# Eight differential attention heads: the gates of a head are computed one head later, the filler is spread 32 or 40 pieces to a head, and tanh, low halves and weight splits change places

## What is computed

```python
h = rms_norm_2(x, norm_g)
(c_glu, c_gate, d_q, d_k, d_v, d_gate, x_q, x_gate, merge) = split(h @ w_in)
u = a * sigmoid(b)              # a, b = split(c_glu): the GLU, then a convolution of 31 taps
u = conv(u, dw) + dw_b
q, k = rms_norm_2(d_q), rms_norm_2(d_k)          # per head: two halves m of 64
s = q @ k.T * scale - slope * dist               # causal
a = softmax(s[0]) - lam * softmax(s[1])
o = rms_norm_2(a @ v, subln_g) * (1 - lambda_init) * silu(d_gate)
```

## Time and profile before

| what | us |
|---|---|
| three runs: median (lowest to highest) | 1282.93 (1280.54 to 1284.0) |
| the profiled execution, its own time | 1289.19 |
| its span from first to last instruction | 1287.4 |
| TensorE busy in the span | 1215.9 (94%) |
| VectorE busy | 867.2 (67%) |
| ScalarE busy | 604.0 (47%) |
| mean granted TensorE clock | 0.973 |

### The profile page before, as it was taken

How to read it: one execution, slowest core, us unless ns; L and a number is a source line. 1 busy time by engine, 2 the same in 40 slices (tenths; PEclk the granted TensorE clock), 3 DMA queues, 4 the chain that set the end, 5 groups by cost and what they waited for, 6 DMA issues and landing times. The chain is left out here.

```text
span 1287.4 us, 17196 instructions
## 1 busy us (share of the span) xinstructions
PE 1215.9 (94%) x6530; PEld 1027.2 (80%) x6530; DVE 867.2 (67%) x1433; ACT 604.0 (47%) x1085; POOL 63.9 (5%) x62
## 2 busy tenths in 40 slices
PE   5999999998889999999999989999999899999998
PEld 5998888886689997777777766788887688788888
DVE  5887666757747246777977796588777668763341
ACT  6644364544546455664666455332564321752230
POOL 2039000000000000000000000000000000000001
PEclk9989999999989999999999999999999899999999
DMA  9965222110055322122112213223321422332211
GB/s 356 357 226 169 73 66 66 53 47 17 23 218 202 99 83 73 42 66 82 66 33 66 82 49 131 78 87 103 94 66 50 146 67 99 98 99 98 99 66 50
DMA packets 34290, 130.24 MB, mean 101 GB/s; under 512 B 4000, under 2 KB 4256, under 8 KB 33696
## 3 DMA queue, kind: packets, MB, share of 16 engines
q1 hardware_dynamic: 30672, 111.69, 26.2%
q0 software_dynamic: 3248, 17.14, 3.6%
q10 hardware_dynamic: 288, 0.31, 0.1%
HBM read 122.83 MB, written 6.29 MB: 100 GB/s over the span
## 5 line engine op out<-in xcount | busy, mean ns | idle before, releaser
L433 PE MATMUL bank<-hl,wh 128*128 128x512 f32 x880 | 365.7, 416 | 8.0 <-ACT th L1062 5.3
L434 PE MATMUL bank<-hh,wl 128*128 128x512 f32 x880 | 348.6, 396 | 0.0
L435 PE MATMUL bank<-hh,wh 128*128 128x512 f32 x880 | 348.6, 396 | 0.0
L1015 ACT ACTIVATE wh<-raw 128x1024 fp32r<-128x1024 f32 x187 | 192.1, 1054 | 205.3 <-PE bank L435 193.1
L1647 DVE TENSOR_TENSOR wl<-raw,wh 128x1024 fp32r<-128x1024 f32 x187 | 227.0, 1239 | 85.4 <-ACT wh L1015 84.6
L433 PEld LDWEIGHTS bank<-hl,wh 128*128 128x128 f32 x880 | 168.9, 192 | 46.9 <-issue 13.2
L435 PEld LDWEIGHTS bank<-hh,wh 128*128 128x128 f32 x880 | 168.6, 192 | 37.4
L434 PEld LDWEIGHTS bank<-hh,wl 128*128 128x128 f32 x880 | 169.0, 192 | 35.2 <-issue 4.4
L2078 DVE SCALAR_TENSOR_TENSOR ca<-u,vt,ca 128x512 f32<-128x512 f32 x232 | 157.9, 745 | 0.0
L433 PE MATMUL bank<-wl,hh 128*128 128x256 f32 (+1 forms) x352 | 101.8, 289 | 3.1 <-DVE hl L2333 2.4
L434 PE MATMUL bank<-wh,hl 128*128 128x256 f32 (+1 forms) x352 | 100.0, 284 | 0.0
(11 more groups left out here) (315 smaller groups left out, 1971.7 us busy)
## 6 DMA issues: line engine op xcount, KB each, us to landing
raw<-in_chunks SPq DMA_DIRECT2D x195, 512.0 KB, 3.7
ada_a<-in_chunks SPq DMA_DIRECT2D x8, 512.0 KB, 12.8
ada_b<-in_chunks SPq DMA_DIRECT2D x8, 512.0 KB, 12.8
x<-in_x POOLq DMA_DIRECT2D x4, 512.0 KB, 10.7
mem_scratch<-kvm POOLq DMA_DIRECT2D x1, 2048.0 KB, 8.2
x<-in_x POOLq DMA_DIRECT2D x1, 2048.0 KB, 9.5
x_scratch<-x POOLq DMA_DIRECT2D x1, 2048.0 KB, 6.6
kvm<-mem_scratch POOLq DMA_DIRECT2D x1, 2048.0 KB, 8.7
```

Of the source, the lines that this page charges most:

```text
L433: pe.matmul(o, a[0], b[1], start=start, stop=False, **kw)
L434: pe.matmul(o, a[1], b[0], start=False, stop=False, **kw)
L435: return pe.matmul(o, a[0], b[0], start=False, stop=stop, **kw)
L1015: act.activation(wh[:, SLOT[nxt]], raw[:, RAW_SLOT[nxt]], ACT.Copy).then_inc(s.w_hi, 1)
```

## The change

Seven edits, all in the stage of the eight heads:

1. The gate `dg` of head j becomes filler of head j + 1, ahead of that head's `gb` and `ga`; `dg` of head 7 stays in head 7, last.
2. Head 0 has 32 pieces instead of 40 and head 7 has 32 instead of 24; both give 8 to each tile.
3. At tt = 0 the turn of the previous head's last unit is two pieces later on TensorE.
4. ScalarE does its tanh ahead of the exponentials: of `dg(j - 1)` at tt = 2, of `gb(j)` at tt = 3 (before: behind them, `gb` at tt = 2, `dg` at tt = 3). In head 7 these are at tt = 1 and 2.
5. The high and low of the transposed probabilities come directly behind the exponentials and behind `prob`, ahead of weight splits, readouts and roots.
6. On VectorE the GLU of head j moves from tt = 3 to tt = 0 of head j + 1, the gate from tt = 3 to tt = 2, the mix from ahead of `prob` to behind it, and the output's low from tt = 3 to tt = 0 of the next head. In head 7 the mix and both output halves stay at tt = 3, behind `prob`.
7. Four taps move from tt = 2 to tt = 1; head 1 has four taps fewer, and the later stage runs 10 instead of 9 behind each projection chunk.

```diff
-    CHUNKS += [("gb", _j), ("ga", _j), ("dg", _j)]
+    CHUNKS += ([("dg", _j - 1)] if _j else []) + [("gb", _j), ("ga", _j)] + ([("dg", 7)] if _j == 7 else [])
...
-                    at, half = (10 * tt, 5) if j < 7 else ((0, 8, 12, 16)[tt], (4, 2, 2, 4)[tt])
+                    at, half = (10 * tt, 5) if 0 < j < 7 else (8 * tt, 4)
...
-                    if tt < 3 and 4 * j + tt > 0:
+                    if tt in (1, 2):
                         diff_turn(4 * j + tt - 1)
                     pieces(fill, at + half, 2)
-                    if tt == 3:
+                    if tt in (0, 3) and 4 * j + tt > 0:
                         diff_turn(4 * j + tt - 1)
...
+                    if j and tt == (2 if j < 7 else 1):
+                        tanh_of(("dg", j - 1)).then_inc(s.tanhed, 1)
+                        th_free[0] = ("dg", j - 1)
                     if tt == 3:
                         if j < 7:
                             act.wait_ge(s.qn_done, 2 * j + 4)
                             split_head(j + 1, ("D", u_, 1))
+                    if tt == (3 if j < 7 else 2):
+                        banks.empty(tanh_of(("gb", j)), ("gb", j))
+                        th_free[0] = ("ga", j)
...
+                    if u_ > 0:
+                        diff_pt_hi(u_ - 1)
...
+            ahead(("ga", 7))
             gate_of(("dg", 7))
             diff_pt_hi(31)
...
+                    if tt == 0 and j > 0:
+                        glu(j - 1)
+                    if (j, tt) == (7, 3):
+                        glu(7)
...
-                    if tt == 3 and j > 0:
-                        diff_mix(j - 1)
+                    if tt == 0 and j > 1:
+                        dve.wait_ge(s.mixed, j - 1)
+                        split_o(j - 2, 7 + j)
                     if tt < 3:
-                        conv(4, j)
+                        conv(4, j if tt else j - 1)
...
+                    if u_ > 0:
+                        diff_pt_lo(u_ - 1)
...
-            branch("d", diff_tail, lambda: conv(9, 8))
+            branch("d", diff_tail, lambda: conv(10, 8))
```

More of the change, by code:

```diff
@@ L771, in _ @@
             for j in range(8):
-                fill = ([("dq", j + 1), ("dk", j + 1)] if j < 7 else []) + [("gb", j), ("ga", j), ("dg", j)]
+                fill = [("dq", j + 1), ("dk", j + 1)] if j < 7 else []
+                fill += ([("dg", j - 1)] if j else []) + [("gb", j), ("ga", j)] + ([("dg", 7)] if j == 7 else [])
                 for tt in range(4):
-                    at, half = (10 * tt, 5) if j < 7 else ((0, 8, 12, 16)[tt], (4, 2, 2, 4)[tt])
+                    at, half = (10 * tt, 5) if 0 < j < 7 else (8 * tt, 4)
                     pieces(fill, at, half)
@@ L1448, in _ @@
                     if tt == 0 and j > 0:
-                        ahead(("dg", j - 1))
+                        ahead(("ga", j - 1))
                     if tt < 2 and j < 7:
@@ L1454, in _ @@
                         square_q(tt)
[L1455 to L1461, removed]
+                    if tt == 2 and j < 7:
+                        roots_together(([("sub", j - 1)] if j else []) + [("dns", 2 * j + 2 + i) for i in range(2)],
+                                       norms[:, 0:3 if j else 2, :])
                     if tt == 2:
                         split_v(dv[:, :, j * P:j * P + P], ("DO", j - 1) if j else ("PO", 15))
-                        ahead(("gb", j))
[L1465 to L1470, removed]
+                    if tt == 2 and j == 7:
+                        roots_together([("sub", 6)], norms[:, 2:3, :])
+                    if j and tt == (2 if j < 7 else 1):
+                        ahead(("dg", j - 1))
+                    if tt == (3 if j < 7 else 2):
+                        ahead(("gb", j))
+                    if tt == 3 and j > 0:
+                        split_o(j - 1, last=("wp", 3, 1), mixed=j)
+            ahead(("ga", 7))
             gate_of(("dg", 7))
@@ L2085, in conv, with glu @@
                         dve.tensor_tensor(u[:, j, PAD:], ca[:, 0, :], ca[:, 1, :], ALU.add).then_inc(s.conv_done, 1)
+            def glu(j):
+                key = ("ga", j)
+                banks.wait_empty(dve, ("gb", j))
+                banks.wait_full(dve, key)
+                banks.empty(dve.scalar_tensor_tensor(u[:, j, PAD:], th[:], 1.0, bank(key)[:], ALU.add, ALU.mult), key)
             def diff_pt_lo(u_):
@@ L2114, in _ @@
                            .then_inc(s.negmax, 1)
+                    if j and tt == (2 if j < 7 else 1):
+                        if j > 1:
+                            dve.wait_ge(s.mixed, j - 1)
+                        gate_to(("dg", j - 1), gj[:], False)
                     if tt == 3 and j < 7:
@@ L2132, in _ @@
                        .then_inc(s.prob_ready, 1)
+                    if u_ > 0:
+                        diff_pt_lo(u_ - 1)
                     if tt == 0 and j > 0:
-                        banks.wait_full(dve, ("dg", j - 1))
-                        ahead(("dg", j - 1))
+                        banks.wait_full(dve, ("ga", j - 1))
+                        ahead(("gb", j - 1))
+                        ahead(("ga", j - 1))
                     if tt < 2 and j < 7:
@@ L2139, in _ @@
                         ahead(key)
[L2140 to L2145, removed]
                     if tt == 2:
                         split_v(6 + j, dv[:, :, j * P:j * P + P])
[L2148 to L2157, removed]
+                        if j < 7:
+                            norm_q(0, v("dqn"), ("dns", 2 * j + 2))
+                            norm_q(1, v("dkn"), ("dns", 2 * j + 3))
+                    if tt == 1:
+                        conv(4, j)
+                    if j and tt == (2 if j < 7 else 1):
+                        ahead(("dg", j - 1))
+                    if tt == 3 and j > 0:
+                        diff_mix(j - 1)
+                    if (j, tt) == (7, 3):
+                        dve.wait_ge(s.mixed, 7)
+                        split_o(6, 15)
+                    if (j, tt) == (7, 2):
+                        banks.wait_full(dve, ("gb", 7))
+                        ahead(("gb", 7))
+            ahead(("ga", 7))
             gate_to(("dg", 7), gj[:])
```

## The result

The changed kernel takes 1265.89 us in the median of four runs (1264.09 to 1269.03), the kernel before 1283.47 in the same job; the ratio is 0.9854 with an interval of 0.983 to 0.9878. In a later job it took 1267.49 against 1283.3 (0.9861, 0.9832 to 0.989). Forecast were 1263 and 20 less; it is 16 to 18 less. The profiled execution took 1266.38 (span 1264.6).

What follows compares the result with a forecast made beforehand. TensorE, busy 94% of the span, waited mostly for VectorE's low at the turns. Gains of 15.6 + 7 + 0.95 less 0.8, 1.2 and 1.5 gave 20.0, from 1282.93 to 1262.9, said as 1263; range 1256 to 1272.

Steps and rivals of the forecast that it cites:

- The chain at the boundary: From tile 2 to the next head's turn: VectorE's low ends at 17.2 instead of 20.35, the turn comes at 19.4.
- The boundaries: Seven turns between heads no longer wait for VectorE's low: 15.6 us gained.
- Head 0: At head 1's start, behind a head 0 with fewer pieces, a new wait for the tanh: 0.8 us lost once.
- Inside head 7: Eight more pieces partly cover head 7's two waits: 1.15 left against 2.1, 0.95 us gained.
- The end: Behind head 7, in front of diff_values(7): a wait of 3.6 against 2.4 before, 1.2 us lost.
- Waits in sum: TensorE's waits over the stage of the heads: 20.1 to 5.6, 14.6 us less.
- The clock: Lower-clock stretches behind the stalls go, 7 us back; one returns behind the last wait, 1.5 us lost.
- The rival in which the stalls go and the clock doesn't come back: Boundary stalls vanish but the lower-clock stretches stay in the runs: gain 14.5, 1268.4 us, chance 25%.
- the forecast's own range: Whole kernel: the forecast itself holds from 1259.5 to 1267 us, chance 52%.
- The difference between 1289.19 and the median: Kernel before: runs without a profile 6.3 us faster than the profiled execution, about the 7 the clock costs in it.

Runs made afterwards that it cites:

- The tanh experiment: Changed kernel with the tanh of gb at tile 3 put back behind the exponentials in heads 0 to 6: 1275.1 us, ratio 0.9915 to before.
- the links: Changed kernel with three or eight extra multiplications of prob by 1.0 on VectorE, ahead of the low at tile 3 of heads 0 to 6: 1270.2 and 1289.1 us.
- the two single edits of the kernel before: Kernel before with prob and low ahead of mix and gate at tile 3: 1283.9 us; or with tile 0's turn two pieces later: 1275.6 us.
- the kernel with all three order edits: Kernel before with low first at tile 3, turn two pieces later, and every high and low ahead of splits and readouts: 1273.6 us.
- The first experiment: Changed kernel with the high and low of unit 31 ahead of weight splits and gate behind head 7: 1260.5 us; again 1260.7.
- The low-first run: Kernel before with prob and the low made ahead of the mix and gate on VectorE at tile 3: 1283.9 us, ratio 0.9999.
- the kernel with the turn later: Kernel before with the turn at tile 0 two pieces later on TensorE: 1275.6 us, ratio 0.9941.
- three links: Changed kernel with three extra multiplications of prob by 1.0 on VectorE ahead of the low at tile 3, heads 0 to 6: 1270.2 us.
- eight links: Changed kernel with eight extra multiplications of prob by 1.0 on VectorE ahead of the low at tile 3, heads 0 to 6: 1289.1 us.

## Why the prediction was right, and where it was off

**The chain at the boundary: shown.** Counted from VectorE's first maximum of head 4's tile 2 (633.71 here), the timeline of the changed kernel, VectorE:

```profile
642.63 0.69 DVE L1793 TENSOR_TENSOR vv<-dv,vv 128x512 fp32r<-128x512 f32 x1 [2.94 <-ACT vv L1237]
...
645.70 1.28 DVE L2126 TENSOR_REDUCE stat<-bank 128x1 f32<-128x512 f32 x2
...
648.93 0.17 DVE L2145 RECIPROCAL stat<-stat 128x2 f32<-128x2 f32 x1
...
650.51 0.55 DVE L1843 TENSOR_TENSOR ptl<-bank,pth 128x384 fp32r<-128x384 f32 x1
...
652.36 0.68 DVE L2099 SCALAR_TENSOR_TENSOR u<-th,bank 128x512 f32<-128x512 f32 x1
```

ScalarE and TensorE:

```profile
635.70 0.69 ACT L1035 ACTIVATE norms<-bank,sc 128x512 f32<-128x512 f32 x1
636.49 1.28 ACT L1042 ACT_TABLE_LOAD   x1
637.78 1.49 ACT L1042 ACTIVATE norms<-norms 128x1536 f32<-128x1536 f32 x1
...
646.51 0.60 ACT L1063 ACTIVATE th<-bank 128x512 f32<-128x512 f32 x1
```

```profile
647.32 0.41 PE L433 MATMUL bank<-hl,wh 128*128 128x512 f32 x1
...
653.08 0.60 PE L628 MATMUL bank<-cst,prob 128*128 128x128 f32 x4
```

`vv` is at 8.9 (forecast 8.75), the maxima at 12.0 (11.8), the reciprocal at 15.2 (15.05), the low ends at 17.35 (17.2), the GLU begins at 18.65 (18.5), the turn at 19.4 (19.4). All of VectorE is 0.15 later than forecast, because the first table load stands 0.79 behind the mean's start and not 0.62. So the spares are 2.0 at the turn, 1.3 at the GLU, and 0.2 at the tanh, which ends at 13.4 for a piece at 13.6. The tanh experiment and the links put a price on the last two. The load is 1.29 before its activation here too, and no drain shows; by the Trainium skill ("ScalarE: Activation LUTs", What ACT_TABLE_LOAD costs) there would be 1.38 more to each, and the trace disagrees.

**The boundaries: 15.6 forecast, 15.6 measured** (all seven waits are gone). What the prediction didn't see is how the edits hang together. It credited the gain to mix, gate and GLU leaving the chain; the two single edits of the kernel before show that each alone passes a part of the wait, or most of it, to the next turn. The timeline of the first shows the three splits in front of the late low there, and the kernel with all three order edits has no such wait. So the low ahead of the splits, to which the prediction gave no value, was most likely needed as well; the first two edits together without it were not run.

**Head 0: 0.8 lost forecast, 0.93 measured. Inside head 7: 1.15 left forecast, 0.64 measured** (no wait at `subln`). **The end: 3.6 forecast, 4.0 and 0.3 at the turn measured**, against 2.4 before; from the end of unit 30's low to that of the last one it is 761.08 to 767.85, 6.8 against 6.7. The first experiment shows that the queue of splits was the cause.

**Waits in sum:** 14.6 less forecast (20.1 to 5.6), 14.2 less in the profile. Span times clock says 14.4, and 15.0 in the later job.

**The clock is the term that was mis-sized.** Forecast were 7 back and 1.5 lost, 5.5 in all. In the two traces it came about so: the stage's five stretches at the lower clock are gone, for 7 to 8 us, and one follows the wait of 4.0. But the profiled execution of before had a clock of 0.973, at the lowest end of that kernel's runs, whose median was 0.980. In the runs the clock takes (1 - 0.980) x 1281.8 = 25.6 before and (1 - 0.983) x 1264.1 = 21.5 after, so it gives 4 and not 5.5; and this is rough, as the four runs after lie between 0.976 and 0.984. In the later job the clock is 0.979 for both, so it gives 0.3, and the waits alone make the 15.8. The medians thus show 0 to 4 us.

The rival in which the stalls go and the clock doesn't come back named this, and its 1268.4 was as near as the forecast's 1263 in the first job (2.5 and 2.9 off) and much nearer in the second (0.9 and 4.5 off, with 1267.5 just above the 1267 at which the forecast's own range ended). The mechanism of the waits was right; that the first number fell inside that range is in part luck. The difference between 1289.19 and the median was itself the sign: I named it in the rival and didn't use it in the sum. It isn't a cost of being profiled, as the rival supposed: of the twelve profiled executions of the kernels here but before, five are faster than their kernel's median. The low-first run says the same as the rival: it lost most of the stage's stretches in its profile, and its runs gained nothing in clock.

Not settled: what decides how many stretches at the lower clock an execution has. It doesn't simply follow the waits: the kernel with the turn later has 16.8 us of waits and 0.985, the one with three links 7.9 and 0.981.

## What to carry to other kernels

- Between two meetings of two engines the order within one engine's queue moves a wait from one meeting to the next. Before costing a reorder, list the next two things that the waiting engine asks for and where they stand in the same queue: here two edits that took 1.5 and 2.0 us from each boundary gave 0.3 to 1.5 of it to the turn behind, and 3 to 4 us in the last head.
- Put what another engine waits for first, and work with long notice (weight splits three chunks ahead) last, also behind the last iteration: one line moved on each of two engines there was worth 5 to 7 us.
- Take a profiled execution's clock beside the clocks of the runs. What the lower clock costs in the one profile is not what a change gives back in the median.

## What the runs showed of the hardware that was not expected

- In the profiled executions the stretches at half rate ahead of the heads differ where TensorE's work is the same: the clock there was 0.96 before and 0.97 after, with 3.8 us between them, and the eight profiles of the changed kernel and its variants reach head 1's first piece at 491.13 to 496.78 us.
- Runs of one kernel differ by up to 9 us (1281.45 to 1290.6 of before in the last job; 1280.02 to 1288.29 in the first), and their granted clock goes along with it: in the first, 0.983 for the shortest and 0.975 for the longest.
- The stall of 2.46 us was followed by a stretch at 1.2 GHz in four of its five places in the profile of the kernel before; with 0.5 and 1.5 us in its place (low first), or 1.0 and 0.5 (turn later), none stood in heads 1 to 6; with 1.7 and 0.7 (eight links), one did of five, and a wait of 2.37 in head 7 of that kernel had none behind it. So a stall of this length makes the lower clock likely, and doesn't settle it. Even the same wait of 4.0 us had a stretch behind it that was twice as long in one profile of the changed kernel as in the other.
- A short wait of TensorE costs more than its own length: 0.22 us made a head 0.5 longer, and 1.11 us 1.35, at a clock of 1.00 throughout.
